# Four-row-tile chunks of an fp32 product kernel: the first two and last two weight pieces of a chunk multiplied row tile by row tile

## The reference

```python
def hybrid_layer(x, ctx, ...):            # x, ctx: 256 x 2048 each
    shift, scale, gate = silu(c) @ w_ada + b_ada        # the same for c_ctx
    h  = rms_norm(x, norm_w)   * (1 + scale) + shift
    hc = rms_norm(ctx, norm_w) * (1 + scale_c) + shift_c
    p  = h @ w_in                         # 2048 x 6144: pool v, pool gate, q, k, v, attention gate
    pc = hc @ w_in                        # layer 0: all columns; layer 1: only k and v
    ... rms norm of q and k, rotary, differential softmax attention, pooling ...
    x_new = x + gate * (concat(pool_o, attn_o) @ w_out) # layer 0: also ctx_new
```

## The kernel before

| chunk | start, us | of what | beside it |
|---|---|---|---|
| 1 to 4 (layer 0) | 227.3, 270.8, 314.4, 359.1 | k, v, q, k | nothing on TensorE but two L596 groups; adaLN sums on VectorE |
| 5 to 12 (layer 0) | 403.8, 449.9, 508.8, 567.8, 618.4, 676.0, 735.9, 790.0 | v, q, pool v (2), pool gate (2, SiLU), attention gate (2, SiLU) | the attention of layer 0, then pooling |
| `w_out` of layer 0 | 839.8 | two tiles, banks 0 and 1 | closing work |
| 13 to 16 (layer 1) | 1081.4, 1124.9, 1169.9, 1215.7 | k, v, k, v | adaLN sums in 13 and 14, attention in 15 and 16 |

## Time and profile before

### The profile page before, as it was taken

One profiled execution on the slowest core, in us unless ns is written; L12 is line 12 of the kernel. 1 busy time (PEld: TensorE's weight loads), 2 busy tenths in 40 slices (PEclk: granted clock), 3 DMA queues, 4 the chain that ended last, 5 costly groups with the idle time before them and its releaser, 6 DMA issues.

```text
span 3414.9 us, 43820 instructions
## 1 busy us (share of the span) xinstructions
PE 3394.9 (99%) x15986; PEld 2777.0 (81%) x15986; DVE 2265.3 (66%) x2757; ACT 1641.7 (48%) x2142; POOL 218.2 (6%) x407
## 2 busy tenths in 40 slices
PE   8999999999999999999999999999999999999999
PEld 6778877778888877888888888888888888888887
DVE  5659977767687657565467774656545687777644
ACT  6442244443354245545555554444454566666443
POOL 1010111101100100100011000000000000000000
PEclk9999999999999999999999999999999999999999
DMA  9978845557867735767777676765654666666665
GB/s 376 400 237 273 281 142 181 180 177 251 272 197 249 266 115 191 243 191 211 218 240 235 203 241 204 251 215 185 210 172 149 189 186 193 189 190 187 205 192 167
DMA packets 331821, 738.84 MB, mean 216 GB/s; under 512 B 26423, under 2 KB 27025, under 8 KB 328448
## 3 DMA queue, kind: packets, MB, share of 16 engines
q1 hardware_dynamic: 298496, 620.83, 57.1%
q0 software_dynamic: 30640, 106.22, 8.7%
q10 hardware_dynamic: 2512, 9.45, 0.8%
HBM read 691.19 MB, written 45.21 MB: 216 GB/s over the span
## 4 chain that ended last, share of the span: by engine, by line
PE 97%; DMA 1%; DVE 1%; ACT 1%; issue 0%; SPq 0%; POOL 0%; ACTq 0%; DVEq 0%; POOLq 0%
PE psum L734 30%; PE psum L736 29%; PE psum L735 29%; PE psum L1310 1%; PE psum L1333 1%; DMA w_raw<-xa_w_k 1%; PE psum L1319 1%; PE psum L1377 1%; PE psum L560 0%; PE psum L2161 0%; PE psum L806 0%; PE psum L2316 0%; PE psum L2018 0%; PE psum L2329 0%; PE psum L1291 0%; PE psum L1362 0%
## 5 line engine op out<-in xcount | busy, mean ns | idle before, releaser
L631 DVE TENSOR_TENSOR w_lo<-w_raw,w_hi 128x1024 fp32r<-128x1024 f32 x997 | 1217.6, 1224 | 974.0 <-ACT w_hi L623 970.8
L623 ACT ACTIVATE w_hi<-w_raw 128x1024 fp32r<-128x1024 f32 x997 | 1052.4, 1059 | 1271.3 <-PE psum L736 1156.3
L734 PE MATMUL psum<-w_hi,a_hi 128*128 128x512 f32 x3072 | 1214.3, 395 | 1.8 <-ACT stage L657 1.1
L736 PE MATMUL psum<-w_hi,a_lo 128*128 128x512 f32 x3072 | 1197.3, 390 | 0.0
L735 PE MATMUL psum<-w_lo,a_hi 128*128 128x512 f32 x3072 | 1195.7, 389 | 0.0
L734 PEld LDWEIGHTS psum<-w_hi,a_hi 128*128 128x128 f32 x3072 | 577.0, 188 | 123.1 <-issue 4.5
L736 PEld LDWEIGHTS psum<-w_hi,a_lo 128*128 128x128 f32 x3072 | 576.6, 188 | 122.1
L735 PEld LDWEIGHTS psum<-w_lo,a_hi 128*128 128x128 f32 x3072 | 577.4, 188 | 115.9
L581 DVE SCALAR_TENSOR_TENSOR ada_sum<-ada_raw,cond_st,ada_sum 128x1024 f32<-128x1024 f32 x240 | 299.7, 1280 | 9.8 <-DMA ada_raw<-w_ada 5.4
L734 PE MATMUL psum<-w_hi,f_hi 128*128 128x512 f32 x704 | 275.0, 391 | 0.0
L736 PE MATMUL psum<-w_hi,f_lo 128*128 128x512 f32 x704 | 274.1, 389 | 0.0
(11 more groups left out here) (390 smaller groups left out, 2829.9 us busy)
## 6 DMA issues: line engine op xcount, KB each, us to landing
w_raw<-w_in SPq DMA_DIRECT2D x416, 512.0 KB, 4.4
ada_raw<-w_ada SPq DMA_DIRECT2D x176, 512.0 KB, 5.9
w_raw<-ffn_w_up SPq DMA_DIRECT2D x176, 512.0 KB, 3.7
w_raw<-w_out SPq DMA_DIRECT2D x96, 512.0 KB, 4.4
w_raw<-ffn_w_down SPq DMA_DIRECT2D x88, 512.0 KB, 3.9
p<-stage POOLq DMA_DIRECT2D x152, 256.0 KB, 4.5
w_raw<-xa_w_k SPq DMA_DIRECT2D x32, 512.0 KB, 9.1
w_raw<-xa_w_v SPq DMA_DIRECT2D x32, 512.0 KB, 8.3
```

The source lines that it names most:

```text
L623: nc.scalar.activation(w_hi[:, slot], raw_of(k), ACT.Copy).then_inc(hi_ready, 1)
L631: nc.vector.tensor_tensor(w_lo[:, slot], raw_of(k), w_hi[:, slot].bitcast(F32), ALU.subtract).then_inc(lo_ready, 1)
L734: nc.tensor.matmul(acc, g.hi[:, tt, kt, :], w_hi[:, slot, kk, :], start=first, stop=False)
L736: mm = nc.tensor.matmul(acc, g.lo[:, tt, kt, :], w_hi[:, slot, kk, :], start=False, stop=last)
```

## The change

Only the order of TensorE's program changes. In chunks with four row tiles (the first chunk of each layer's set, number 1 and 13, is left out) pieces 1 and 2 are taken as a pair, and pieces 7 and 8: both pieces for row tile 1, then both for tile 2, 3 and 4. The step of other work that belonged behind the pair's first piece now comes after row tile 2, the second one after row tile 4 as before. What hangs on a piece (`ring_used`, adaLN matmuls) comes after its row tile 4, so for the first piece of a pair between the two pieces of tile 4. The number of matmuls and of steps stays as it was; each call of `piece_pe` has its wait for the low part, so there are more waits.

```diff
                 elif j == g.per_chunk - 1:
                     mm.then_inc(acc_ready, 1)
+            if tiles and tiles[-1] != g.tiles - 1:
+                return
             for a in g.ada.get(k, ()):
                 ada_pe(pe, a)
...
         LAST_PIECES = 3
+        OPENERS = (plan["lanes0"][0], plan["lanes1"][0])
...
-            for j in range(g.per_chunk - by_tile):
-                piece_pe(pe, g, i, c, j)
+            def stepped(j):
                 if woven:
                     advance(woven, rate, start, i * g.body_pieces + c * g.per_chunk + j)
+
+            coupled = ()
+            if g.tiles == 4 and woven:
+                coupled = () if g in OPENERS else (0, g.per_chunk - 2)
+            done = 0
+            for j in range(g.per_chunk - by_tile):
+                if j < done:
+                    continue
+                if j in coupled:
+                    for tt in range(g.tiles):
+                        for jj in (j, j + 1):
+                            piece_pe(pe, g, i, c, jj, [tt])
+                        if tt == 1:
+                            stepped(j)
+                    stepped(j + 1)
+                    done = j + 2
+                    continue
+                piece_pe(pe, g, i, c, j)
+                stepped(j)
```

## The result

The changed kernel takes 3431.94 us (median of 6 runs, 3430.12 to 3433.23) against 3416.99 (6 runs, 3416.44 to 3417.47). The ratio is 1.0043, with a 95% interval of 1.0033 to 1.0053: slower by 15.0 us. Its profiled execution is 3432.70 us with a span of 3431.0.

What follows compares the result with a forecast made beforehand. TensorE, 97% of the chain, bounds the kernel; added stops of 2.7 + 0.2 + 2.7 + 1.0 + 1.6 + 3.8 = 12.0 us take profiled execution from 3416.54 to 3428.5, the median to 3429.0, range 3424 to 3435.

Steps and rivals of the forecast that it cites:

- A pair costs nothing in itself: All pairs: matmul and step counts stay, added waits for low parts are already satisfied, so they cost nothing.
- (c): Chunk 5, preparation of q and k: transposes wait 0.6 us at piece 7 and 0.4 at piece 8, together 1.0.
- (a): Ends of chunks 2, 3, 4, 12: late PSUM copies stop TensorE 0.67 us each, 2.7 together; after chunk 15, 0.2.
- (b): Ends of chunks 9 and 10, with ScalarE's table load: each stop 2.12 us instead of 0.77, together 2.7 more.
- (d): After chunk 12: VectorE's adaLN sums come behind its low part, so TensorE's transposes come later, costing 1.6 us.
- (e): After chunk 14: L596 waits for VectorE's last sums, late behind the low part; 3.8 us, the largest term.
- rival (4): Half clock set off again by the stop after chunk 14, at most half of 5.6 us lost: 3431.8; 8 in 100.
- The forecast's own upper end, 17: Whole kernel: highest added cost in us, with (c) at 3, (d) at 2.3 and 2 us for cover that fails.
- the waits for L657: Sign in the changed kernel's profile: TensorE's waits there grow from 2 to about 7 stops, some 7 us.
- L1312 waits for VectorE: Sign in the changed kernel's profile: this line, L1291 before the change, waits for VectorE twice.

Runs made afterwards that it cites:

- e9: Changed kernel with copies of tiles 1 to 3 ahead of ScalarE's cast, and adaLN sums ahead of the low part only ending chunks 12 and 14; 3416.32 us.
- e3: Changed kernel without the pair at the end of chunk 14; 3425.68 us.
- e2: Changed kernel with only the last two pieces of a chunk paired, no start pairs; 3430.83 us.
- e1: Changed kernel with only the first two pieces of a chunk paired, no end pairs; 3417.96 us.
- e6: Changed kernel with VectorE's adaLN sums ahead of the low part at the second piece of every pair; 3426.71 us.
- e4: Kernel before the change with one pair alone, at the end of chunk 14; 3423.92 us.
- e5: Changed kernel with ScalarE's copies of row tiles 1 to 3 ahead of the cast at a paired chunk's last piece; 3424.70 us.

## Why the prediction was right

The forecast was 3429.0 in a range of 3424 to 3435, slower by over 0.2%; it came out at 3431.94. Its terms, one by one:

- *A pair costs nothing in itself.* Held. Chunks 7, 8 and 11 have pairs at both ends and last as before to 0.01, and e9, with all pairs, runs at the time of the kernel before, 0.6 below it, with the two old stops (1.6) gone and step (c) left. A pair's only price is what it makes other engines late by.
- *(a) Bare chunk ends,* forecast 0.67 each: 0.71 each, 0.59 before the next chunk's first matmul and 0.12 behind it (the forecast had 0.08). After chunk 15, forecast 0.2: 0.26 in e3, where no low clock covers it. Sum 3.1 against 2.9.
- *(b) Ends of 9 and 10,* forecast 1.35 each: 1.32 and 1.34 in e2, 1.33 and 1.34 in e3. The drain that the Trainium skill adds (ScalarE: Activation LUTs, What ACT_TABLE_LOAD costs) was not seen: with it each end would have been 1.4 longer, and the trace's own 2.40 from cast to copy gave the sum.
- *(c) Preparation,* forecast 0.6 + 0.4: 0.65 + 0.25 in e1. Both parts in their place; the second was taken too high by 0.15.
- *(d) After chunk 12,* forecast 1.6: 1.5, which is the 1.63 of the table less the 0.12 that the stop after chunk 12 leaves behind (with the sums moved, e6, 0.13 is what stays there). *(e) After chunk 14,* forecast 3.8: 3.77.
- The sum, forecast 12.0, measured 11.9 in the profile.

So the mechanism holds at every place, and the experiments show it by removal: with the copies ahead of the cast (a) and (b) go, with the sums ahead of the low part (d) and (e) go, without the start pairs (e2) (c) goes, and with both reorderings in the right places the time is that of the kernel before.

What was wrong in it is one step, the price and the chance of **rival (4), the clock**. It was put at 8 in 100 and tied to the stop in (e), at most 2.8 us. It happened behind two stops, one of them (b)'s at chunk 9, and cost 3.2 us in the profiled execution. The error was to treat it as a case beside the forecast, where it is a likely term on top of the stops: in the profiles it follows the stop of 3.7 us in four of four executions (the change, e2, e4, e5), and those at the ends of chunks 9 and 10 once in eight. 12.0 from the stops on 3417.0 gives 3429.0, and each of the six runs lay 1.1 to 4.2 above that (with what the start of the run adds or takes). The row for it stood there but was read as the price of the long stop at the start alone. The Trainium skill (TensorE: Matmul & The Clock Gate, HAM oscillation) says that idle gaps between bursts bring the lower clock back; the trace now agrees, with shares of 0.53 and 0.62 behind a stop of 3.7 us. The forecast's own upper end, 17, would have covered the measured 15.0, but by luck: it was made of a larger (c), a larger (d) and cover that fails, and none of these came.

Two signs named in the prediction came out smaller: the waits for L657 are 6 and not 7, since the one after chunk 15 shows no row of its own, and their idle time is 5.4 and not 7, because the idle time of a row leaves out the 0.16 us of modelled end and the 0.12 of broken beat, 0.28 for each stop; with these the six stops cost 7.1. L1312 waits for VectorE once, as its second wait, 0.25 us in chunk 6, is too short to get a row.

## What to carry to other kernels

When a matmul order is changed, look at which matmul now gives the signal that other engines wait for, and at what stands behind that wait in their queues: here 4.1 us of a later signal cost nothing to the data that it guards, and 12 us to the copies and sums behind it. Moving an instruction ahead of a waiting one needs the same look the other way, whether its own wait (here a DMA, 6.73 us) is safe to stand in front. And a stop of TensorE of a few microseconds in an otherwise full stream can have a spell of low clock behind it (here each stop of 3.7 us had, and one in eight of about 2 us); the sum of the waits in a profile is then too low.

## What the hardware showed that was not expected

- The low clock doesn't need an idle stretch as long as the one at the start. It came behind the stop at the end of chunk 9, where 2.0 us lie between the due start (679.17 + 0.23) and the real one (681.41), behind those of 3.7 us at chunk 14, and behind 0.78 and 1.29 us close together in e5. Behind the stops of 3.7 us it came in all four profiled executions that have one. Behind the shorter ones it is the exception: the stop at chunk 9 went without it in e2, e3 and e6, the equal one at chunk 10 in all four, and so did the place behind chunk 12 in the change, e2 and e3.
- Its cost for one stop at chunk 14 was 1.6 us in the change and 2.5 in e4, where it fell while TensorE still stood (0.67 at 1172 to 1174) and not once it was at work again.
- Matmuls whose result is thrown away, put into the stop, kept the clock at 1.00 and took 3.1 us off the time (3423.92 to 3420.85), though TensorE waits just as long for its data.
